# mLSTM's weighted scores times values as two fp32r products of split operands, values padded to 130 columns

## What is computed

```python
dmat = jnp.where(causal, bcum[..., :, None] - bcum[..., None, :] + ig[..., None, :], -jnp.inf)
m_t = jnp.maximum(m_inter, jnp.max(dmat, axis=-1))
w = jnp.einsum('bhtd,bhsd->bhts', q, k) * jnp.exp(dmat - m_t[..., None])
num = jnp.einsum('bhts,bhse->bhte', w, v) + ...          # the carried state
den = jnp.sum(w, axis=-1) + ...
h = num / jnp.maximum(jnp.abs(den), jnp.exp(-m_t))[..., None]
```

## Time and profile before

| | us |
|---|---|
| median of 3 runs (lowest, highest) | 1465.67 (1465.5, 1465.68) |
| the profiled execution, its own time | 1466.68 |
| its span (first to last instruction of the core) | 1464.9 |
| PE busy | 1454.1 |
| DVE busy | 1105.3 |
| ACT busy | 748.0 |
| POOL busy | 425.7 |

### The profile page before, as it was taken

How to read it: one execution, slowest core, us unless ns; L and a number is a source line. 1 busy time by engine, 2 the same in 40 slices (tenths; PEclk the granted TensorE clock), 3 DMA queues, 4 the chain that set the end, 5 groups by cost and what they waited for, 6 DMA issues and landing times.

```text
span 1464.9 us, 22285 instructions
## 1 busy us (share of the span) xinstructions
PE 1454.1 (99%) x7466; PEld 1207.3 (82%) x7466; DVE 1105.3 (75%) x1902; ACT 748.0 (51%) x955; POOL 425.7 (29%) x200
## 2 busy tenths in 40 slices
PE   8999999999999999999999999999999999999999
PEld 7888777878788888888888888888888888888887
DVE  4977688877589999996999997346666666666665
ACT  6444677477645455554556555454444444444442
POOL 5866435436546687884000000000000000000000
PEclk9999999999999999999999999999999999999999
DMA  6544633438433666666888888988898888888883
GB/s 239 164 144 152 202 123 108 166 127 301 153 116 111 219 219 209 216 209 206 299 303 303 308 300 304 325 282 283 300 294 284 294 284 295 283 296 282 297 284 140
DMA packets 166561, 345.16 MB, mean 236 GB/s; under 512 B 13404, under 2 KB 78940, under 8 KB 164192
## 3 DMA queue, kind: packets, MB, share of 16 engines
q1 hardware_dynamic: 166496, 344.32, 69.0%
HBM read 268.76 MB, written 75.51 MB: 235 GB/s over the span
## 4 chain that ended last, share of the span: by engine, by line
PE 86%; DVE 10%; ACT 2%; POOL 1%; issue 0%; DMA 0%; SPq 0%; POOLq 0%; ACTq 0%; DVEq 0%
PE ps L1224 32%; PE ps L1215 25%; PE ps L744 9%; PE ps L767 6%; PE ps L1253 4%; PE ps L1084 3%; DVE top_lists L2149 1%; DVE top_lists L2142 1%; POOL u_r L537 1%; PE ps L949 1%; PE ps L732 1%; DVE top_in L2143 1%; DVE top_lists L2146 1%; DVE top_lists L2139 1%; PE ps L933 1%; PE ps L959 1%
## 5 line engine op out<-in xcount | busy, mean ns | idle before, releaser
L1215 PE MATMUL ps<-hT_r,u_r 128*128 128x512 f32 x2048 | 470.6, 390 | 0.1
L1224 PE MATMUL ps<-v_r,w_pairs 128*128 128x512 f32 x2036 | 461.7, 389 | 0.0
L1215 PEld LDWEIGHTS ps<-hT_r,u_r 128*128 128x128 f32 x2048 | 382.7, 188 | 79.8 <-POOL u_r L537 0.5
L1224 PEld LDWEIGHTS ps<-v_r,w_pairs 128*128 128x128 f32 x2036 | 382.3, 188 | 79.2
L490 POOL TENSOR_TENSOR w_r<-w_raw,w_r 128x1024 fp32r<-128x1024 f32 x85 | 216.5, 2553 | 183.6 <-ACT w_r L1332 108.6
L2288 DVE TENSOR_TENSOR v_r<-vraw,v_r 128x1024 fp32r<-128x1024 f32 x128 | 156.8, 1225 | 147.3 <-ACT v_r L1670 147.3
L1670 ACT ACTIVATE v_r<-vraw 128x1024 fp32r<-128x1024 f32 x128 | 136.0, 1062 | 253.5 <-PE ps L1224 248.1
L1617 ACT ACTIVATE act_stage<-ps 128x512 f32<-128x512 f32 x128 | 76.7, 600 | 226.3 <-PE ps L1215 226.2
L537 POOL TENSOR_TENSOR u_r<-uraw,u_r 128x1024 fp32r<-128x1024 f32 x60 | 173.1, 2896 | 46.5 <-ACT u_r L1598 46.2
L1332 ACT ACTIVATE w_r<-w_raw 128x1024 fp32r<-128x1024 f32 x95 | 100.1, 1060 | 111.1 <-PE ps L744 43.1
L1598 ACT ACTIVATE u_r<-uraw 128x1024 fp32r<-128x1024 f32 x128 | 134.9, 1054 | 15.9 <-DMA uraw<-in_u 15.8
(11 more groups left out here) (272 smaller groups left out, 1538.4 us busy)
## 6 DMA issues: line engine op xcount, KB each, us to landing
uraw<-in_u SPq DMA_DIRECT2D x128, 512.0 KB, 4.7
vraw<-in_v SPq DMA_DIRECT2D x128, 512.0 KB, 5.1
w_raw<-in_w SPq DMA_DIRECT2D x101, 512.0 KB, 3.5
acts_out<-act_stage SPq DMA_DIRECT2D x128, 256.0 KB, 2.3
gates<-stage SPq DMA_DIRECT2D x16, 2048.0 KB, 7.4
g_in<-gates SPq DMA_DIRECT2D x64, 512.0 KB, 6.4
act_in<-acts_out SPq DMA_DIRECT2D x128, 256.0 KB, 5.1
gates_pre<-pre_stage SPq DMA_DIRECT2D x24, 256.0 KB, 2.4
```

Of the source, the lines that this page charges most:

```text
L1215: ins = pe.matmul(bank(s % 2), u2[s][:, w, k * P:(k + 1) * P], hr4[:, w, k, :], start=i == 0, stop=i == 15, skip_group_check=True)
L1224: ins = pe.matmul(bank(2 * q + h), w2[:, s, w, q * P:(q + 1) * P], v2[s][:, w, h * BANK:(h + 1) * BANK], start=start and w == 0, stop=stop ...
```

## The change

The values product is done as the scores already are: two fp32r products per block, high with high and low with low. On ACT `high_v(t)` copies each of the four value tiles scaled by KEEP to fp32r, and POOL's `low_v(t)` subtracts that from the values and writes the low part in place. For each head, DVE's `weigh` (now with SPREAD once more in its factor) is followed by ACT's `high_e(h)`, the high part of the 1280 weighted scores scaled by 1/SPREAD, and DVE's `low_e(h)`, the low part. `ml_values` waits for the split values and for `low_e`. The values get 130 columns a head in place of 129, both extra ones set to 1, and the areas behind them move by 16 columns. On DVE decay(3) now comes ahead of take_gate(16), and split_low(2) directly behind it, ahead of weigh(0). Some semaphores are merged with no change of order (`if_ln` and `thr_made` into `if_made`; `qk_squared` and `ml_squared` into `squared`; `qk_rooted` into `rooted`).

```diff
-        ml_v = carve("ml_v", 32768, TT * MLH * (HD + 1))
+        ml_v = carve("ml_v", 32768, TT * MLH * (HD + 2))
+        aw_r = carve_r("aw_r", 45088 + 2 * CAUSAL, 2 * CAUSAL)
+        ml_v_low = carve_r("ml_v_low", 32768, TT * MLH * (HD + 2))
+        ml_v_high = [carve_r(f"ml_v_high{t}", at, MLH * (HD + 2)) for t, at in enumerate((43040, 43560, 44080, 30720))]
...
+        ew_hi = [lkr[0][h % 2] for h in range(MLH)]
+        ew_lo = [lkr[1][0], lkr[1][1], aw_r[:, 0:CAUSAL], aw_r[:, CAUSAL:2 * CAUSAL]]
...
# POOL
+            def low_v(t):
+                pool.wait_ge(v_split_hi, t + 1)
+                n = MLH * (HD + 2)
+                at_least(pool, v_split_lo, t)
+                pool.tensor_tensor(ml_v_low[:, t * n:t * n + n], ml_v[:, t * n:t * n + n],
+                                   ml_v_high[t].bitcast(F32), ALU.subtract).then_inc(v_split_lo, 1)
+
             for h in range(MLH):
                 pool.wait_ge(e_ready, h + 1)
                 keep_causal(ew[h], e_masked)
+                if h < 2:
+                    low_v(2 * h)
+                    low_v(2 * h + 1)
...
# PE
+                pe.wait_ge(v_split_lo, TT)
                 pe.wait_ge(w_ready, h + 1)
                 for t in range(TT):
-                    at = (h % 2 * 3 + t // 2) * BANK + (t % 2) * (HD + 1)
+                    at = (h % 2 * 3 + t // 2) * BANK + (t % 2) * (HD + 2)
                     for kt in range(t + 1):
-                        ins = pe.matmul(ps[:, at:at + HD + 1], part(ew[h], kt, t, t + 1), ml_v4[:, kt, h, :],
-                                        start=kt == 0, stop=kt == t)
+                        for w, weights in enumerate((ew_hi[h], ew_lo[h])):
+                            ins = pe.matmul(ps[:, at:at + HD + 2], part(weights, kt, t, t + 1),
+                                            ml_v_parts[w][kt][:, h * (HD + 2):(h + 1) * (HD + 2)],
+                                            start=kt + w == 0, stop=kt == t and w == 1)
...
# ACT
+            def high_v(t):
+
+                n = MLH * (HD + 2)
+                act.activation(ml_v_high[t], ml_v[:, t * n:t * n + n], ACT.Copy, scale=KEEP).then_inc(v_split_hi, 1)
+
+            def high_e(h):
+
+                act.wait_ge(weighed, h + 1)
+                at_least(act, num_done, h - 1)
+                act.activation(ew_hi[h], ew[h], ACT.Copy, scale=1.0 / SPREAD).then_inc(weighed_hi, 1)
...
                 act.activation(ew[h], ew[h], ACT.Exp, scale=-1.0).then_inc(e_ready, 1)
                 if h == 0:
+                    act.wait_ge(cols_turned, 1)
+                    for t in range(TT - 1):
+                        high_v(t)
+                if h == 1:
                     split_high(MLH - 1)
+                    act.wait_ge(y_done, PAIRS)
+                    high_v(TT - 1)
+            for h in range(2):
+                high_e(h)
             high_ws(I_G + 18, I_G + 19)
             act.activation(ml_o, ml_o, ACT.Sigmoid).then_inc(ml_factors, 1)
-            high_ws(I_G + 20, I_G + 21, I_G + 22)
+            high_ws(I_G + 20)
+            for h in range(2, MLH):
+                high_e(h)
+            high_ws(I_G + 21, I_G + 22)
...
# DVE
             decay(2)
+            decay(3)
             take_gate(16)
-            decay(3)
+            split_low(2)
 
             def weigh(h):
                 dve.wait_ge(e_masked, h + 1)
                 dve.wait_ge(s_ready, h + 1)
-                dve.scalar_tensor_tensor(out=ew[h], in0=region(h % 2), scalar=HD_SCALE * SPREAD, in1=ew[h],
-                                         op0=ALU.mult, op1=ALU.mult).then_inc(w_ready, 1)
+                dve.scalar_tensor_tensor(out=ew[h], in0=region(h % 2), scalar=HD_SCALE * SPREAD * SPREAD, in1=ew[h],
+                                         op0=ALU.mult, op1=ALU.mult).then_inc(weighed, 1)
+
+            def low_e(h):
+                dve.wait_ge(weighed_hi, h + 1)
+                dve.scalar_tensor_tensor(out=ew_lo[h], in0=ew_hi[h].bitcast(F32), scalar=1.0 - SPREAD, in1=ew[h],
+                                         op0=ALU.mult, op1=ALU.add).then_inc(w_ready, 1)
...
             for h in (0, 2):
                 weigh(h)
                 weigh(h + 1)
+                low_e(h)
+                low_e(h + 1)
                 take_gate(17 + h)
-                if h == 0:
-                    split_low(2)
                 divide(h)
                 divide(h + 1)
```

More of the change, by code:

```diff
@@ L182, in build @@
         sb_v = carve("sb_v", 30720, 2048)
-        ml_v = carve("ml_v", 32768, TT * MLH * (HD + 1))
-        ml_o = carve("ml_o", 34832, 2048)
-        mem_q = carve("mem_q", 36880, 2048)
-        y_sbT = carve("y_sbT", 38928, 2048)
+        ml_v = carve("ml_v", 32768, TT * MLH * (HD + 2))
+        ml_o = carve("ml_o", 34848, 2048)
+        mem_q = carve("mem_q", 36896, 2048)
+        y_sbT = carve("y_sbT", 38944, 2048)
         y_mlT = carve("y_mlT", 22528, 2048)
[L188 to L193, removed]
+        y_memT = carve("y_memT", 43040, 2048)
+        rows = carve("rows", 40992, 4096)
+        wf_raw = carve("wf_raw", 50208, KD * MLH)
+        r_all = carve("r_all", 40992, 2048)
+        work = carve("work", 45088, 5120)
+        memT_r = carve_r("memT_r", 46112, 4096)
         tri_r = carve_r("tri_r", 50704, P)
@@ L200, in build @@
         rstd_b = carve("rstd_b", 51344, T)
-        w_y = carve_r("w_y", 36880, 4096)
+        w_y = carve_r("w_y", 36896, 4096)
         rstd_p = carve("rstd_p", 31744, T)
@@ L276, in build @@
         sb_v3 = sb_v.rearrange("p (t c) -> p t c", c=512)
-        ml_v4 = ml_v.rearrange("p (t h c) -> p t h c", t=TT, c=HD + 1)
+        ml_v4 = ml_v.rearrange("p (t h c) -> p t h c", t=TT, c=HD + 2)
+        ml_v_parts = (ml_v_high, [ml_v_low[:, t * MLH * (HD + 2):(t + 1) * MLH * (HD + 2)] for t in range(TT)])
         ml_o3 = ml_o.rearrange("p (t c) -> p t c", c=512)
@@ L411, in build @@
             sem("num_out"))
-        ml_squared, ml_factors, ml_normed, mlT_done, mlT_out = (
-            sem("ml_squared"), sem("ml_factors"), sem("ml_normed"), sem("mlT_done"), sem("mlT_out"))
+        ml_factors, ml_normed, mlT_done, mlT_out = (
+            sem("ml_factors"), sem("ml_normed"), sem("mlT_done"), sem("mlT_out"))
         qkT_done, qkT_out = sem("qkT_done"), sem("qkT_out")
@@ L903, in turn_rows @@
             def turn_rows():
-                pe.wait_ge(thr_made, 1)
+                pe.wait_ge(if_made, 2)
                 pe.wait_ge(y_out, PAIRS - 1)
@@ L1398, in _ @@
             high_w(I_N + 2, (I_N + 2) % 4)
-            act.activation(r_abs, r_abs, ACT.Ln, bias=1.0).then_inc(if_ln, 1)
+            act.activation(r_abs, r_abs, ACT.Ln, bias=1.0).then_inc(if_made, 1)
             for b in range(4):
@@ L1408, in _ @@
                 high_w(n, n % 4)
-            act.wait_ge(qk_squared, 2)
+            act.wait_ge(squared, 3)
             act.activation(roots[:, S_Q:S_ML], sums[:, S_Q:S_ML], ACT.Sqrt, bias=eps_col[:, :],
-                           scale=1.0 / HD).then_inc(qk_rooted, 1)
+                           scale=1.0 / HD).then_inc(rooted, 1)
             high_w(I_G + 4, (I_G + 4) % 4)
@@ L1458, in _ @@
                     act.wait_ge(rows_made, 1)
-                    act.activation(r_m, r_m, ACT.Exp, scale=-1.0).then_inc(thr_made, 1)
+                    act.activation(r_m, r_m, ACT.Exp, scale=-1.0).then_inc(if_made, 1)
                 if p < PAIRS - 1:
@@ L1848, in norm_q @@
             def norm_q():
-                dve.wait_ge(qk_rooted, 1)
+                dve.wait_ge(rooted, 3)
                 link(dve.reciprocal(rstd[:, S_Q:S_ML], roots[:, S_Q:S_ML]))
```

28 lines of the change are left out of this document (14 added, 14 removed).

## The result

The kernel became slower: 1474.43 us median of 6 runs (1473.29 to 1475.86) against 1465.68 (1465.5 to 1467.09), ratio 1.0059 (95% interval 1.0049 to 1.0069), +8.75 us. The forecast was 1470.2, slower by 4.5, with 1471.8 as the upper bound. The profiled execution took 1474.37 us with a span of 1472.6, 7.7 above the span of before, and the mean granted clock is 0.996.

What follows compares the result with a forecast made beforehand. TensorE, busy 99% of the span, was taken to bound the kernel; stalls of 2.70 and 1.81 us and 0 for the products made +4.5 on 1465.67, 1470.2 us. Stated range 1466.2 to 1471.8.

Steps and rivals of the forecast that it cites:

- Bound by TensorE: Whole kernel: TensorE is busy 99% of the span, so its loss or gain in this stage reaches the end nearly one to one.
- The price of a product, 0.11 us: Value products: each fp32r product of 130 columns takes 0.11 us start to start, the weight load included.
- Gain on PE: 0: Value products: 80 fp32r products take 8.8 us, as the 80 records before; bounds 0 and 4.0 us.
- the rival with short products: Value products cost 0.06 us each, so the second pair's take 2.4 us instead of 4.4; +0.8 us, 1466.5; 9%.
- First stall, 2.70 us: Gate item 17 waits for its bank: decays alternate with POOL's subtractions, take_gate(16) ends at 261.31; TensorE loses 2.7 us.
- the bound that I had named and not taken: Decays beside POOL: DVE's last decay instruction slips in front of low_v(3), the chain is 0.7 us shorter, +3.8 in all.
- Second stall, 1.81 us: First value product waits for split_low(2), weighing, high_e(0) and low_e(0), starting 1.81 us after TensorE is ready.
- The second pair of heads: Scores and values of heads 2 and 3: no stall, 0.5 us to spare, and no gain.
- The sum: Whole kernel: stalls of 2.70 and 1.81 us plus 0 for the products give +4.5 us, 1470.2 us.
- more than counted: Rival: a further wait of POOL's or ACT's queue in the second pair, above 1472.2 us; 4%.
- own range: The forecast case's own bounds, 1469.3 to 1472.2 us, from a shorter decay chain to costlier subtractions.

Runs made afterwards that it cites:

- products_130: Kernel before, its order and waits kept, value products exchanged for two fp32r products of 130 columns a block from stand-in operands; 1466.62 us against 1465.95.
- fill_both: Changed kernel plus 7 extra 512-column fp32r products before gate item 17 and 9 before the first value product, filling idle TensorE; 1470.39 us against 1466.07 before.
- low_on_act: Changed kernel without GpSimd's four value subtractions; ScalarE writes scaled copies as the low tiles instead (result incomplete); 1466.86 us against 1465.80 before.
- fill_first: Changed kernel plus only the 7 extra products before gate item 17, the second idle stretch left; 1475.39 us against 1466.07 before.
- fill_second: Changed kernel plus only the 9 extra products before the first value product, the first idle stretch left; 1469.82 us against 1466.07 before.
- order: Changed kernel with VectorE's old order: take_gate(16) ahead of decay(3), split_low(2) behind take_gate(17); 1474.60 us against 1465.95 before.
- fp32_waits: Changed kernel, splits and waits kept, value products plain fp32 of 130 columns, one a block, from the low parts alone; 1470.67 us against 1466.07 before.
- products_64: Kernel before, its order and waits kept, value products exchanged for two fp32r products of 64 columns a block from stand-in operands; 1469.56 us against 1465.95.
- low_act_order: Changed kernel with ScalarE's scaled copies in place of GpSimd's four value subtractions and VectorE's old order; 1469.39 us against 1465.80 before.
- pool_only: Kernel before plus four GpSimd subtractions of 520 columns between its masks, into unused space, nothing else changed; 1470.59 us against 1465.80.

## Why the prediction was right or wrong

**Bound by TensorE.** Right: the stage's +9.14 less the 1.3 of its earlier start is the span's 7.7 to 0.1 us, and nothing behind the stage gave any of it back. That the sum closes on the span's 7.7 and not on 9.1 goes back to the early fall of the clock in the trace of before; it is an accident of that execution.

**The price of a product, 0.11 us.** Right: 0.111 at full clock in the changed kernel, 0.110 in products_130, and the load as its cause by 64 and 256 columns and by the cheaper bf16 load. One step of the reading was wrong: 222 against 275 ns is not half, and the fp32r products of products_130 have a median of 275 ns too, so medians of records don't compare the two forms. "Gain on PE: 0" held; the rival with short products is dead.

**First stall, 2.70 us.** The mechanism was right (decays in turns with the subtractions, take_gate(16) late, gate item 17 waiting for its bank), the size 1.80. Of the 0.9 between, 0.7 is the bound that I had named and not taken: the last decay instruction slipped in front of low_v(3) (VectorE's last one ends at 258.48, and GpSimd's subtraction runs until 259.63).

**Second stall, 1.81 us.** Right in kind; 2.39. What the first lost came back here: split_low(2) then waited for low_v(3). The two together were forecast at 4.51 and measured 4.19, and fill_both puts 4.3 on the medians. That the subtractions cause them is shown by low_on_act.

**The second pair of heads.** Right: +0.04 us, no wait.

**The sum, and where it failed.** The sum added two stalls and priced everything that runs behind them as before ("So TensorE is 2.70 + 1.81 = 4.5 us later at gate item 18", and nothing more). The missing term is the granted clock: with 1.65 and 2.20 us of idle and then 40 products that by the estimate above stream for half their time, TensorE ran at 1.2 GHz for about 10 us and lost 2.70 + 2.21 = 4.9 us, 4.0 by the medians of the changed kernel and fill_both. I had read 0.999 as a property of the kernel and carried it over. In the trace of before it is a fall between 10 and 20 us, far from this stage, and the kernels above show that the clock in a stage depends on the work and the waits in it. I also had a row on the shorter streaming in hand, the 222 ns, and used it for the pace alone. What in the sequence brings the clock down is narrowed and not settled: filling the idle stretches keeps it up, plain fp32 products behind them mostly do. None of the rivals held this; "more than counted" named a further wait.

**"More than counted" and the range.** The own range ended at 1472.2, for costlier subtractions, the stated one at 1471.8. Both were bounds on waits, so they could not hold a term of another kind.

## What to carry to other kernels

When weights change with every product, two products with half the streaming cost as much as one with double: compare the distance between the starts of short products, never their durations, before giving an operand a cheaper type. In a kernel that TensorE bounds, price an idle stretch of a few us together with what runs behind it: a train of short products there can double its cost, and filling the idle time with useless full products took 4.0 of 8.75 us back. One profile shows one execution: where the clock varies between runs, read each run's clock before a median's rest is put down to anything else. And before work goes to a GpSimd that seems free, list which VectorE instructions with SBUF inputs stand beside it, and again wherever its later work then comes to lie.

## What the runs showed of the hardware that was not expected

- In the traces the granted clock fell to 1.2 GHz after 1.65 to 3.2 us of idle TensorE with short fp32r products or a gate item behind it (the changed kernel, fill_first, fill_second, order), and didn't after the same idle with fp32 products behind it (fp32_waits, whose other runs lost 0.6 us to the clock in the mean). After a fall it lasted until well into work that kept PE busy: gate item 18 took 5.95 us for 3.74.
- The clock varies between executions of one kernel: 0.997 to 1.000 in the ten runs of fill_second, 0.994 to 0.999 in the four of fill_first and the eight of products_64.
- Short fp32r products alone, without any idle time, can do it: 64 columns to each load, 3.6 us on the median, and by the runs' clocks an estimated 4.0. With 130 columns and no idle it did not show in the profile, and the median was within the interval of no change.
- TensorE's stage began about 1 us later in the seven traces with a clock of 0.83 between 10 and 20 us, the trace of before among them. One profile's span carries that, so the stages were compared, not the ends.
- VectorE and GpSimd took turns instruction by instruction: where the decays' eight VectorE instructions met four subtractions of GpSimd's and its masks, the two decays took 5.44 us for 2.60. Instructions with two SBUF inputs are held up as well: split_low(2) took 2.27 and 2.88 us beside GpSimd's weight subtractions (low_act_order), 0.67 and 0.68 without (low_on_act). The Trainium skill's page "SBUF — State Buffer", section "Who interferes with whom", states the lock, and these rows agree; that a held-up instruction moves the next meeting elsewhere is what low_act_order and pool_only add, 2.1 and 2.3 us.
